# Grouping the token gather of a mixture-of-experts kernel by four pairs, with a longer loop and other places for y

## The reference

```python
def one_block(args):                       # routed: 64 experts, 8 per token
    t, g, ex = args
    h = x_pad[t] @ w_gate_up[ex]           # 1024 -> 2*256
    h = jax.nn.silu(h[:, :256]) * h[:, 256:]
    return (h @ w_down[ex]) * g[:, None]   # 256 -> 1024
...
def shared_expert(x_flat, w_gate_up, w_down):
    h = x_flat @ w_gate_up
    return (jax.nn.silu(h[:, :256]) * h[:, 256:]) @ w_down
...
x = layer_norm(alpha * x + shared + routed)
```

## Time and profile before

| what | us |
|---|---|
| median of three runs | 1458.78 (1458.64 to 1459.03) |
| the profiled execution, its own time | 1459.04 |
| its span | 1457.2 |
| TensorE busy in the span | 1426.3 (98%) |
| VectorE / ScalarE busy | 545.8 / 458.7 |
| granted TensorE clock, mean | 0.997 |

### The profile page before, as it was taken

One profiled execution on the slowest core, in us unless ns is written; L12 is line 12 of the kernel. 1 busy time (PEld: TensorE's weight loads), 2 busy tenths in 40 slices (PEclk: granted clock), 3 DMA queues, 4 the chain that ended last, 5 costly groups with the idle time before them and its releaser, 6 DMA issues.

```text
span 1457.2 us, 23728 instructions
## 1 busy us (share of the span) xinstructions
PE 1426.3 (98%) x10072; PEld 867.6 (60%) x10072; DVE 545.8 (37%) x880; ACT 458.7 (31%) x735; POOL 32.8 (2%) x30
## 2 busy tenths in 40 slices
PE   9999999999999999999999999999999999999996
PEld 8999998544444444434389999984334344333442
DVE  4577856321212212111355778562121221221124
ACT  4565444222122221112155644432222122221212
POOL 0011000000000000000001010000000000000000
PEclk9999999999999999999999999999999999999998
DMA  9763588599999999999955445786999999999995
GB/s 313 232 212 132 195 315 355 212 427 425 426 425 424 427 423 426 423 427 425 362 192 193 155 174 228 293 318 256 426 425 425 424 426 424 427 423 425 425 421 206
DMA packets 83988, 498.81 MB, mean 342 GB/s; under 512 B 6384, under 2 KB 11760, under 8 KB 51888
## 3 DMA queue, kind: packets, MB, share of 16 engines
q1 hardware_dynamic: 82176, 495.75, 84.2%
q10 hardware_dynamic: 1712, 1.57, 0.4%
HBM read 494.95 MB, written 1.05 MB: 340 GB/s over the span
## 4 chain that ended last, share of the span: by engine, by line
PE 79%; DMA 14%; DVE 2%; ACT 2%; SPq 2%; issue 1%; DVEq 0%
PE bank L1765 27%; PE bank L1595 14%; PE bank L1796 12%; DMA arena<-in_expert_w_gate_up 11%; PE bank L1707 5%; PE bank L1736 4%; PE bank L1660 4%; PE bank L1543 3%; PE bank L1479 2%; DMA ring_w<-in_w_in 1%; PE bank L1779 1%; ACT w_hi L751 1%; PE bank L1519 1%; PE bank L1728 1%; DMA ring_w<-in_w_out 1%
## 5 line engine op out<-in xcount | busy, mean ns | idle before, releaser
L1595 PE MATMUL bank<-x_hi,w_hi 128*128 128x256 f32 x704 | 201.3, 286 | 1.6 <-DVE w_lo L990 1.0
L1595 PE MATMUL bank<-x_lo,w_hi 128*128 128x256 f32 x704 | 199.2, 283 | 0.0
L1595 PE MATMUL bank<-x_hi,w_lo 128*128 128x256 f32 x704 | 199.2, 283 | 0.0
L990 DVE TENSOR_TENSOR w_lo<-ring_w,w_hi 128x2048 fp32r<-128x2048 f32 x69 | 158.0, 2290 | 102.6 <-ACT w_hi L751 102.4
L1402 DVE SCALAR_TENSOR_TENSOR y_lo<-bank,slot_info,y_hi 128x512 fp32r<-128x512 f32 x128 | 96.1, 751 | 208.3 <-ACT y_hi L905 208.3
L1765 PE MATMUL bank<-arena,xe_even 128*64 128x512 f32 x768 | 170.1, 595 | 3.6 <-DMA arena<-in_expert_w_gate_up 3.1
L1765 PE MATMUL bank<-arena,xe_odd 128*64 128x512 f32 x768 | 170.1, 595 | 1.6 <-DMA arena<-in_expert_w_gate_up 1.0
L1390 DVE TENSOR_TENSOR hid<-hid,bank 128x256 f32<-128x256 f32 x64 | 27.0, 421 | 377.1 <-ACT hid L898 377.1
L905 ACT ACTIVATE y_hi<-bank,slot_info 128x512 fp32r<-128x512 f32 x128 | 88.0, 688 | 230.4 <-PE bank L1796 230.4
L898 ACT ACTIVATE hid<-bank 128x256 f32<-128x256 f32 x64 | 24.6, 384 | 414.5 <-PE bank L1765 414.5
L751 ACT CAST w_hi<-ring_w 128x2048 fp32r<-128x2048 f32 x69 | 131.4, 1904 | 68.3 <-PE bank L1660 30.5
(11 more groups left out here) (216 smaller groups left out, 1783.5 us busy)
## 6 DMA issues: line engine op xcount, KB each, us to landing
arena<-in_expert_w_gate_up SPq DMA_DIRECT2D x46, 4096.0 KB, 22.1
gu_c<-in_expert_w_gate_up SPq DMA_DIRECT2D x16, 4096.0 KB, 23.9
ring_w<-in_w_in SPq DMA_DIRECT2D x25, 2048.0 KB, 9.1
dn_a<-in_expert_w_down SPq DMA_DIRECT2D x24, 2048.0 KB, 19.8
arena<-in_expert_w_down SPq DMA_DIRECT2D x22, 2048.0 KB, 19.7
dn_c<-in_expert_w_down SPq DMA_DIRECT2D x16, 2048.0 KB, 22.0
ring_w<-in_w_out SPq DMA_DIRECT2D x4, 2048.0 KB, 11.7
arena<-in_expert_w_gate_up SPq DMA_DIRECT2D x8, 1024.0 KB, 18.1
```

Of the source, the lines that this page charges most:

```text
L990: v.tensor_tensor(chunk_part(w_lo, n), chunk_in(n), chunk_part(w_hi, n).bitcast(F32), ALU.subtract).then_inc(w_lo_ready, 1)
L1595: ins = mm(b[:, S * c:S * c + S], lhs, rhs, start=(k == 0 and a + w == 0), stop=(k == KD - 1 and a == 1))
```

## The change

- Groups are of four pairs throughout (`WIDE = 4`, eight groups): a gather is four matmuls of 256 columns, one k each, a whole PSUM bank; each pair's step has two gathers (2*step behind the up products, 2*step + 1 later). Groups of two and their functions are gone. The bank is full, so the picks go to the first columns of bank 4, and gather 0 of a group waits until `slot_info` of the group before was copied (`gate_s_ready`).
- Pairs 0 to 19 are written out and use three slots; pairs 20 to 27 stand in the loop and 28 to 31 behind it, all on two slots.
- Group 0 is gathered without the shared down products in between; these stand behind pair 0's up products and the first gather of group 1.
- The shared down weights go to the second half of their slot, `x_t` to its first half. `y_hi` lies over `sh_silu` and `sh_t`, `y_lo` over the pooling and router weights.
- So the second layer's `load_params` moves to SyncE's queue behind its block 6, after `acc_done`; and its weight block 1 waits for the last pair's up products in place of `acc_done`.

```diff
-WIDE = 3
-WIDE_GROUPS = 8
+WIDE = 4
...
+GROUPS_OF = PAIRS // WIDE
+FIXED = GROUPS_OF - 3
+def gathers_in(step, following):
+    return ((), ()) if following is None else ((2 * step,), (2 * step + 1,))
...
-        x_t = place("x_t", 24 * KB, [P, KD, S])
-        y_hi = place("y_hi", 28 * KB, [P, D], F32R)
+        x_t = place("x_t", 16 * KB, [P, KD, S])
...
-        y_lo = place("y_lo", 12 * KB, [P, D], F32R)
...
+        place = region("shared_region", 4 * KB)
+        y_hi = place("y_hi", 0, [P, D], F32R)
+        place = region("params_region", 4 * KB)
+        y_lo = place("y_lo", 0, [P, D], F32R)
...
-        PICKED = 480
-        bank_picks = banks[4][:, PICKED:PICKED + 2 * WIDE]
+        bank_picks = banks[4][:, 0:2 * WIDE]
...
-                    dst = ring_w[:, slot, 0:KF * D].rearrange("p (k n) -> p k n", k=KF)
+                    dst = ring_w[:, slot, KF * D:].rearrange("p (k n) -> p k n", k=KF)
...
-                    if (l, n) == (0, 6):
-                        load_params(sp, 0)
+                    if n == 6:
+                        if l:
+                            sp.wait_ge(acc_done, 2 * TT * l)
+                        load_params(sp, l)
...
-                with sp.Fori(0, SHORT_FROM // 3 - 1) as i:
+                with sp.Fori(0, FIXED * WIDE // 3 - 1) as i:
...
-                with sp.Fori(0, short_steps(more) - 1) as i:
-                    pair = 2 * ((i + SHORT_FROM // 2) & (HALVES - 1))
+                with sp.Fori(0, more * (PAIRS // 2) + (PAIRS - FIXED * WIDE) // 2 - 1) as i:
+                    pair = 2 * ((i + FIXED * WIDE // 2) & (PAIRS // 2 - 1))
...
                     load_block(l + 1, 0)
-                    sp.wait_ge(acc_done, 2 * TT * (l + 1))
+                    sp.wait_ge(up_done, 4 * start)
+                    sp.sem_inc(loads_cleared, 1)
                     load_block(l + 1, 1)
...
-                def gather(g, q):
+                def gather(g, q, opening=False):
                     if q == 0:
                         pe.wait_ge(s_ready, g.m + 1 + l)
+                        if not (opening and l == 0):
+                            pe.wait_ge(gate_s_ready, g.m)
...
                     for q in early:
                         gather(following, q)
-                    if not first:
+                    if first:
+                        block_ready(l, BLOCK_OF["shared_down", 0])
+                        for q in range(4):
+                            ins = down_shared(q // 2, q % 2)
+                        ins.then_inc(shared_down, 1)
+                    else:
...
-                block_ready(l, BLOCK_OF["shared_down", 0])
-                for q in range(4):
-                    ins = down_shared(q // 2, q % 2)
-                    gather(triple(start, l, 0), 2 * q)
-                    gather(triple(start, l, 0), 2 * q + 1)
-                ins.then_inc(shared_down, 1)
+                for q in range(KD):
+                    gather(group(start, 0), q, opening=True)
...
+                with pe.Fori(0, loops(more)) as i:
+                    for u in range(PART):
```

More of the change, by code:

```diff
@@ L476, in chunk_part, with loops, loads_before, group @@
             return part if CHUNKS[n][0] == "z" else part.rearrange("p (k a) n -> p k (a n)", k=KW)
[L478 to L502, removed]
+        PART = 2 * WIDE
+        def loops(more):
+            return more * (GROUPS_OF // 2) + 1
+        def loads_before(l, looped, slot):
+            fixed = FIXED * WIDE
+            return l * (fixed // 3) if slot == 2 else l * (fixed // 3 + 3 - slot) + looped
+        def group(start, g):
+            return Group(start + g, KD * start + KD * g, g % 2)
         def norm_std(act, l, which, t):
@@ new lines, in _ @@
+                more = more_rounds(dve, l)
+                with dve.Fori(0, loops(more)) as i:
+                    for u in range(PART):
+                        n = 4 * start + 8 * i + FIXED * WIDE + u
+                        at_group = start + 2 * i
+                        pair_step(n, group(at_group, FIXED + u // WIDE), u % 2, u % WIDE, n - l)
+                        if u % WIDE == WIDE - 1:
+                            picked(group(at_group, FIXED + 1 + u // WIDE), n + 1, 2 * i + FIXED + 2 + u // WIDE)
@@ L1436, in _ @@
+                start = start + more * GROUPS_OF + GROUPS_OF
+                for u in range(WIDE):
+                    n = 4 * start - WIDE + u
+                    pair_step(n, group(start, -1), u % 2, u, n - l, last=u == WIDE - 1)
                 norm_stats(l, 1, 0)
@@ L1814, in _ @@
+                for n in range(FIXED * WIDE):
                     g, step = divmod(n, WIDE)
[L1815 to L1821 removed]
@@ L1830, in _ @@
-                start = start + more * HALVES + HALVES
-                for u in range(2):
-                    pair_step(2 * start - 2 + u, double(start - HALVES, l, 3, 1), u, u, u, loads_before(l + 1, shorts, u), last=u == 1)
-                pe.wait_ge(onehot_t_ready, 2 * start)
-                pe.wait_ge(y_ready, 4 * start - 1)
+                    pair_step(4 * start + n, group(start, g), n % 2, step, n % 3, before[n % 3] + n // 3 + 1,
+                              group(start, g + 1), first=n == 0)
@@ L1836, in _ @@
+                start = start + more * GROUPS_OF + GROUPS_OF
+                for u in range(WIDE):
+                    pair_step(4 * start - WIDE + u, group(start, -1), u % 2, u, u % 2,
+                              loads_before(l, looped, u % 2) + FIXED * WIDE // 3 + u // 2 + 2, last=u == WIDE - 1)
+                pe.wait_ge(onehot_t_ready, 4 * start)
+                pe.wait_ge(y_ready, 8 * start - 1)
                 for half in range(2):
```

179 lines of the change are left out of this document (64 added, 115 removed).

## The result

The changed kernel takes 1462.68 us (median of 8 runs, 1461.51 to 1464.76), the kernel before beside it 1458.74 us (8 runs): ratio 1.0024, 95% interval 1.0015 to 1.0033. That is 3.9 us more. The profiled execution took 1462.83 us, its span is 1460.9, TensorE's mean granted clock 0.991.

The account below looks back on a forecast made before the run. The weight stream (14.80 us a pair) was taken as the bound: later start 2 x 0.7 less tail 2 x 0.1 gave +1.2 us on 1459.04, 1460.2, and 1459.9 us as median; own range 1458 to 1462, outer 1455 to 1465.5.

Parts of the forecast that it names:

- outer range: Whole program: the range that leaves out two in ten runs, 1455 to 1465.5 us.
- own range: Whole program: the forecast's own range, 1458 to 1462 us around 1459.9.
- rival of the dry slots: From pair 20: two slots run dry, some 3 us per layer lost, 1466 us; chance 0.17.
- Wider gathers at nothing: Pairs 1 to 29: TensorE's work falls by 23 us, which becomes waiting for the DMA; costed at nothing.
- Ahead of pair 0: Opening of the expert part: pair 0 starts at 268.1, not 271.38, 3.3 us earlier.
- lower bound: Gathers ahead of pair 0: at ScalarE's pace alone (0.59 us), 0.9 us less.
- The stream's start: Unbroken weight stream, at pair 4's gate/up load: 0.7 us later per layer, between -0.5 and +2.
- The two gaps: Weight stream ahead of pair 3's down load and pair 4's gate/up load: gaps of 1.8 and 2.2 us.
- Two slots from pair 20: Load of pair 20 waits for pair 18, with 2.7 us of cover; cost nothing.
- The tail: Pairs 28 to 31: no gathers, pair 30 still needs its weights; gain 0.1 us per layer, at most 2.1.
- Layer 1's first blocks and parameters at nothing: Layer 1's start: earlier block 1 request and two parameter loads on SyncE's queue change nothing.

Follow-up runs that it names:

- b3: Kernel before with only the gate/up loads of pairs 3 and 4 cut in two, first half issued at half use: 1455.32 us, ratio 0.9971.
- e13: Changed kernel, loads of pairs 3 and 4 cut, tail wait filled, shared down calls spread (one ahead of the gathers, three around pair 0's products): 1455.45 us.
- e3: Changed kernel with eight unused 512-column matmuls filling TensorE's wait for the first one-hot matrix: 1461.79 us, ratio 1.0017.
- e11: Changed kernel with shared down products back between group 0's gathers and eight filling matmuls behind pairs 28 and 29: 1460.21 us, ratio 1.0007.
- e1: Changed kernel with the four shared down calls back between the gathers of group 0: 1461.72 us, ratio 1.0014.
- e4: Changed kernel with one shared down call in the wait for the one-hot matrix, three behind pair 0's up products: 1458.20 us, ratio 0.9999.
- e5: Changed kernel with shared down calls ahead of gathers 0 and 4, two behind pair 0's up products: 1460.19 us, ratio 1.0008.
- e8: Changed kernel with shared calls back between gathers, waits behind pairs 28 and 29 filled, gate/up loads of pairs 3 and 4 cut in two: 1456.54 us.
- e10: Changed kernel with eight unused 512-column matmuls behind the down products of pairs 28 and 29: 1462.48 us, ratio 1.0020.
- e9: Changed kernel with one shared down call ahead of the gathers, three behind pair 0, and filled waits behind pairs 28 and 29: 1457.82 us, ratio 0.9992.
- b1: Kernel before with only the shared down products moved behind pair 0's up products, ahead of the next group's first gather: 1466.06 us, ratio 1.0052.
- b2: Kernel before with shared down products moved behind pair 0's up products and the wait for the one-hot matrix filled: 1459.62 us, ratio 1.0005.

## Why the prediction held, and the step that was short

The time lies within the outer range (1455 to 1465.5) and 2.8 us above the 1459.9 that I gave. It is 0.7 us beyond my own range (1458 to 1462), and the kernel is slower by 0.24%, just over the 0.2% that I called none (the interval starts at 0.15%); slower than that I gave 0.24. The direction and the place of the loss were forecast; of its size, 1.1 us forecast and 3.9 measured, less than a third. That the outer range covers the time owes something to luck: its upper end was drawn for the rival of the dry slots, which did not occur.

- **Wider gathers at nothing: right.** They start 0.12 us apart at the full clock. TensorE is busy 18.3 us less, though two up phases at the low clock add 3.2, so the 23 us of work were about right. The up products wait 14.9 us longer for weights, and the program gains nothing. By the Trainium skill, "TensorE: Matmul & The Clock Gate", section "Back-to-back issue gap", the isolated gap of a matmul of 256 columns is 109 ns by its formula; the rows show 0.12 us, near it. b3 against e13 shows the same from the other side.
- **Ahead of pair 0: the working right, one cost missing.** I gave pair 0 6.75 us from the one-hot matrix (268.1 less 261.35) and pair 1 25.95. With the wait filled they are 6.84 and 25.88 (e3); in the changed kernel 7.69 and 26.71. The step said that the prologue lost what hid in it, and named the wait for the one-hot matrix; it did not say that TensorE, left waiting there for 2.01 us, would do its next gathers at 1.2 GHz. Those are 0.85 us per layer. (The lower bound there was worked out loosely: three cycles of two banks at ScalarE's 0.59 us a copy are 0.7 us less and not 0.9; neither bound was reached at the full clock.)
- **The stream's start: the term that was mis-sized.** +0.7 us per layer was predicted, and up to pair 30 +1.31 and +1.23 measured. The two gaps are where they were put: the issues at 289.33 and 296.41 were predicted at 287.6 and 294.7, of which 1.0 is the later opening and 0.8 the clock. The sum with the measured issue is 296.41 + 1.5 = 297.9 against 295.5, less 1.0 for the opening: +1.4.
- **Two slots from pair 20: right.** Pair 20's load was issued at 529.7 and the windows around 530 show 413 and 431 GB/s. The rival that they run dry has fallen; the trace of e11 leaves at most a few tenths for it.
- **The tail: right in this trace (pair 31 12.7 us behind pair 30), with a cost that I had not seen.** TensorE waits about 2 us before pairs 29 and 30 in place of 0.3. In some executions its clock falls there, and pair 30 takes 1.5 to 1.7 us more. The profiled executions of e1, e3, e4 and e5 have it in both layers, those of e8 to e11 and e13, which fill the wait, in none. How often it strikes the changed kernel no run shows.
- **Layer 1's first blocks and parameters at nothing: right.** From pair 31 of layer 0 to the one-hot matrix of layer 1 there are 276.24 us before (983.52 less 707.28) and 276.47 after (986.06 less 709.59).

In medians, each against its own runs of the kernel before, the 3.9 us are: 1.3 for the longer start of the wide groups and what else e11 keeps, 1.9 for the place of the shared products (e10 less e11; of it e3's trace gives the clock 0.58 and 1.08 us), and 0.7 between the changed kernel and e10, which may be the slow pair 30 or noise. Each is uncertain by about a microsecond. Whether the 0.99 us of the later opening is chance stays open: over all profiles here the first one-hot matrix starts between 260.5 and 263.2 us, with almost the same code ahead of it.

## What to carry to other kernels

Where a stream of loads is the limit, time a change by the last gap in the stream, not by the busy time it removes: here the gap ends when the second pair's up products free their slot. Cutting the first refills in two, so that half of a slot is asked for when half of it is used, gained 3.6 us, where the regrouping gained none. And work that fills a wait on TensorE is worth more than its own time: taking it out can halve the clock of what follows, so leave some of it, or fill the wait.

## What the hardware showed that I had not expected

- A wait of some 2 us on TensorE can be followed by a stretch at 1.2 GHz: granted clock 0.66 over 5 us behind waits of 2.01 us (gathers) and 1.99 us (up products, 8.78 us instead of 7.09). The same wait of 1.99 us left the clock at 1.00 in another execution (7.09 us), and so did e9's 2.77 us ahead of pair 26 (7.09 us). So these traces don't tell which wait will do it. In b1 the low clock lasted longest: 0.50 over 5 us behind a wait of 1.74 us, through the gathers and into the up products, while 1.88 us at the same place of layer 0 did nothing.
- At 1.2 GHz neighbouring gather matmuls start 0.21 to 0.22 us apart, at 192 columns (b1) as at 256, where at 2.4 GHz they were 0.11 and 0.12.
- With the same code, executions can differ by several microseconds together with their mean granted clock (e8, above); but e13's fastest, 1454.03 us, is at 0.994, so the mean clock alone doesn't tell the time. Filling one wait ahead of the gathers brought b1's 0.989 to 0.992 back to b2's 0.996 to 0.997.
